# Sparse attention of a fp32 two-block network: scaled queries, fused add and minimum, row sums by a matmul column, head pairs as 64-row tiles

## The reference, cut to what matters

```python
q = rmsnorm(proj[..., :N_HEADS * dh].reshape(bsz, s, G, HG, dh), q_norm)
gates = jax.nn.sigmoid(proj[..., N_HEADS * dh:])
...
s_c = einsum('bghqd,bgnd->bghqn', qblk, k_c) * scale + head_bias(rel_c)   # 15 compressed keys
o_c = einsum(masked_softmax(s_c, rel_c >= 0), v_c)
...
s_s = einsum('bghqd,bgqkd->bghqk', qblk, k_sel) * scale + bias_s          # selected keys
p_s = masked_softmax(s_s, rel_s >= 0)
o_s = einsum('bghqk,bgqkd->bghqd', p_s, v_sel)
...                                                                       # window: the same with k_w, v_w
return gblk[..., 0:1] * o_c + gblk[..., 1:2] * o_s + gblk[..., 2:3] * o_w
```

## Time and profile before

| what | value |
|---|---|
| median of 3 runs | 1692.65 us |
| the profiled execution: its time, its span | 1695.91 us, 1694.1 us |
| PE busy over the span | 1623.7 us (96%) |
| attention stage from the first query chunk to the first wo_n matmul | 1360.3 to 1477.9 us |
| heads, from one pair to the next | 8.3 us |

### The profile page before, as it was taken

One profiled execution on the slowest core, in us unless ns is written; L12 is line 12 of the kernel. 1 busy time (PEld: TensorE's weight loads), 2 busy tenths in 40 slices (PEclk: granted clock), 3 DMA queues, 4 the chain that ended last, 5 costly groups with the idle time before them and its releaser, 6 DMA issues.

```text
span 1694.1 us, 33532 instructions
## 1 busy us (share of the span) xinstructions
PE 1623.7 (96%) x11620; PEld 1530.7 (90%) x11620; DVE 1096.8 (65%) x1762; ACT 885.5 (52%) x1468; POOL 182.8 (11%) x149
## 2 busy tenths in 40 slices
PE   5899999999999999999999999998999988799999
PEld 5689998977999889998999999888999867799997
DVE  5668666635776666666877666785566737676665
ACT  5476554444655445445446445554545547664443
POOL 5560000065100000000000000000000043300000
PEclk9899999989999999999999999998999989999999
DMA  5216556543465565556665555656455680055554
GB/s 199 87 51 185 184 178 195 166 155 129 160 196 182 186 196 178 184 185 192 195 189 183 187 181 184 203 183 196 150 185 185 202 173 26 1 171 182 181 190 145
DMA packets 81709, 282.80 MB, mean 167 GB/s; under 512 B 8800, under 2 KB 13408, under 8 KB 81632
## 3 DMA queue, kind: packets, MB, share of 16 engines
q1 hardware_dynamic: 77840, 276.88, 50.8%
q10 hardware_dynamic: 3792, 4.85, 1.6%
HBM read 280.12 MB, written 1.57 MB: 166 GB/s over the span
## 4 chain that ended last, share of the span: by engine, by line
PE 89%; DVE 4%; ACT 3%; issue 1%; DMA 1%; ACTq 1%; POOL 0%; SPq 0%; DVEq 0%; POOLq 0%
PE psum L1639 18%; PE psum L1641 18%; PE psum L1640 18%; PE psum L1631 16%; PE psum L1632 9%; PE psum L1767 2%; PE psum L1768 2%; PE psum L1769 2%; ACT arena L847 1%; DMA raw<-tiles 1%; PE psum L2022 1%; PE psum L1929 0%; DMA x<-x_in 0%; DVE arena L1510 0%; DVE xs L986 0%
## 5 line engine op out<-in xcount | busy, mean ns | idle before, releaser
L506 ACT ACTIVATE w_hi<-raw 128x1024 fp32r<-128x1024 f32 x522 | 549.8, 1055 | 479.8 <-PE psum L1641 298.4
L963 DVE TENSOR_TENSOR w_lo<-raw,w_hi 128x1024 fp32r<-128x1024 f32 x468 | 572.0, 1223 | 227.9 <-ACT w_hi L506 227.5
L1639 PE MATMUL psum<-xs,w_hi 128*128 128x256 f32 x1960 | 558.8, 285 | 16.2 <-DVE xs L986 16.2
L1640 PE MATMUL psum<-xs,w_hi 128*128 128x256 f32 x1960 | 556.8, 284 | 0.0
L1641 PE MATMUL psum<-xs,w_lo 128*128 128x256 f32 x1960 | 556.7, 284 | 0.0
L1631 PE MATMUL psum<-hs,w_hi 128*128 128x512 f32 x1216 | 421.8, 390 | 0.0
L1639 PEld LDWEIGHTS psum<-xs,w_hi 128*128 128x128 f32 x1960 | 378.3, 193 | 17.7 <-issue 11.2
L1640 PEld LDWEIGHTS psum<-xs,w_hi 128*128 128x128 f32 x1960 | 378.5, 193 | 0.2
L1641 PEld LDWEIGHTS psum<-xs,w_lo 128*128 128x128 f32 x1960 | 378.4, 193 | 0.0
L1632 PE MATMUL psum<-hs,w_lo 128*128 128x256 f32 x1216 | 342.9, 282 | 0.0
L1631 PEld LDWEIGHTS psum<-hs,w_hi 128*128 128x128 f32 x1216 | 228.3, 188 | 47.6
(11 more groups left out here) (280 smaller groups left out, 1636.6 us busy)
## 6 DMA issues: line engine op xcount, KB each, us to landing
raw<-tiles SPq DMA_DIRECT2D x522, 512.0 KB, 4.1
bias<-bias_dram ACTq DMA_DIRECT2D x8, 256.0 KB, 12.9
x<-x_in SPq DMA_DIRECT2D x1, 1024.0 KB, 8.2
y_out<-x SPq DMA_DIRECT2D x8, 128.0 KB, 3.4
con<-consts SPq DMA_DIRECT2D x1, 771.0 KB, 9.0
bias_dram<-bias_row ACTq DMA_DIRECT2D x1, 512.0 KB, 7.2
row<-rows SPq DMA_DIRECT2D x1, 192.0 KB, 9.2
vec<-vecs SPq DMA_DIRECT2D x1, 80.5 KB, 3.3
```

Source lines behind the costliest of these rows:

```text
L506: act.activation(w_hi[s][:, :], raw[s][:, :], ACT.Copy).then_inc(hi_ready, 1)
L963: dve.tensor_tensor(w_lo[s][:, :], raw[s][:, :], hi_of(w_hi[s][:, :]), ALU.subtract).then_inc(lo_ready, 1)
L1639: pe.matmul(out, w_hi[s][:, c:c + P], x_hi, start=first, stop=False)
L1640: pe.matmul(out, w_hi[s][:, c:c + P], x_lo, start=False, stop=False)
```

## The change

The loop is unrolled into 8 rounds k of two heads (e = 0, 1). Queries are scaled in place before they are turned, by minus the scale; the bias row is negated too, so logits come out negative: the maximum becomes a minimum and Exp takes scale -1. One `tensor_tensor_reduce` adds the bias and leaves the minimum, which is Exp's bias as it stands. `vtok` gets a 65th column of ones for each head and branch, so that the values matmul also gives the row sums; gate and row sum are applied to the output, not the probabilities. The zero-padded copies of the queries are gone: each head's scores use its own 64 rows of the array, e = 0 and e = 1 in turn, into different banks. The gates are Exp, add, reciprocal. POOL adds the branches' outputs. The compressed branch's turn and values, all of group 1's compressed branch and its `turn_queries` move into the rounds.

```diff
@@ gpsimd
-            with pool.Fori(0, HG) as i:
-                for w in range(4):
-                    pool.wait_ge(n_gs, i * 4 + (w + 1))
-                    ... pool.tensor_tensor(probs, probs, n_sc[w]..., ALU.mult) for 2 query blocks
+            for h in range(H):
+                pool.wait_ge(n_od, h + 1)
+                pool.tensor_tensor(both, br[:, :, 0, :], br[:, :, 1, :], ALU.add).then_inc(n_added, 1)
+                pool.wait_ge(n_co, 1 + h // 8)
+                pool.wait_ge(n_added, h + 1)
+                pool.tensor_tensor(no4[:, :, h, :], both, no4[:, :, h, :], ALU.add).then_inc(n_oo, 1)
@@ scalar: nsa
-                split(t0 + RING)
-                (gates: ACT.Sigmoid here)
-                for t in range(t0 + 1, t0 + 4):
+                for t in range(t0, t0 + 4):
                     split(t + RING)
+                def gates():
+                    act.wait_ge(n_gturn, 1)
+                    act.wait_ge(n_root, 1)
+                    (2 x ACT.Exp of 48 columns, scale=n_nr)
-                def queries(i, j):
-                    (4 copies of 64x256 for each two heads)
+                def exps(k, e):
+                    h = 2 * k + e
+                    act.wait_ge(n_log, h + 1)
+                    if k:
+                        act.wait_ge(n_pT, 2 * (h - 2) + 2)
+                    for tb, (a, z) in enumerate([(0, P), (P, 3 * P)]):
+                        for br in range(2):
+                            (ACT.Exp, scale=-1.0, bias=n_mn[h % 4][:, m:m + 1], no accum_out)
                 squares(0)
+                roots(0)
                 split(t0 + 4 + RING)
-                roots(0)
                 queries_turned(0)
+                for t in range(t0 + 5, t0 + 8):
+                    split(t + RING)
                 squares(1)
                 roots(1)
+                for k in range(H // 2):
+                    exps(k, 0)
+                    if k == 0:
+                        gates()
+                    exps(k, 1)
+                    if k in (0, 4):
+                        compressed_exps(k // 4)
+                    probs_turned(k, 0)
+                    probs_turned(k, 1)
+                    if k == 0:
+                        queries_turned(1)
+                    if k in (1, 4):
+                        compressed_turned(k // 4)
@@ vector: nsa
                 def query_scales(g):
+                    then(dve.reciprocal(n_r[...], std[...]))
+                    for tb in range(TB):
+                        dve.tensor_tensor(q, q, r.unsqueeze(2).to_broadcast([P, 8, DH]), ALU.mult).then_inc(n_scaled, 1)
+                def logits(k, e):
+                    h = 2 * k + e
+                    dve.wait_ge(n_s, k + 1)
+                    if k:
+                        dve.wait_ge(n_exp, h - 1)
+                    for tb, (a, z) in enumerate([(0, P), (P, 3 * P)]):
+                        for br in range(2):
+                            dve.tensor_tensor_reduce(out=n_l[e][...], in0=bank(2 * e + br, a, z), in1=table,
+                                                     scale=1.0, scalar=3.0e38, op0=ALU.add, op1=ALU.min,
+                                                     accum_out=n_mn[h % 4][:, m:m + 1])
-                (maxima: tensor_reduce x2, tensor_scalar; scales: reciprocal, tensor_tensor)
+                def outputs(k, e):
+                    dve.wait_ge(n_pv, h + 1)
+                    then(dve.reciprocal(ri.unsqueeze(2), pv[:, :, DH:]))
+                    then(dve.tensor_tensor(sc..., ri..., gate4[:, :, h, 1:3], ALU.mult))
+                    if h >= 4:
+                        dve.wait_ge(n_added, h - 3)
+                    dve.tensor_tensor(n_br[h % 4]..., pv[:, :, 0:DH], sc.unsqueeze(2)..., ALU.mult).then_inc(n_od, 1)
                 evacuate(1)
                 query_sums(1)
+                logits(0, 0)
+                logits(0, 1)
                 query_scales(1)
+                gates()
+                for k in range(H // 2):
+                    if k + 1 < H // 2:
+                        logits(k + 1, 0)
+                        logits(k + 1, 1)
+                    if k in (2, 5):
+                        compressed_outputs(k // 4)
+                    outputs(k, 0)
+                    outputs(k, 1)
+                    if k == 3:
+                        compressed_logits(1)
+                    if k in (1, 4):
+                        compressed_scales(k // 4)
@@ tensor: nsa
                 def turn_queries(g):
-                    pe.wait_ge(out_read, OUT0["nq"] + 2 * g + 2)
+                    pe.wait_ge(n_scaled, 2 * g + 2)
+                def scores(k):
+                    pe.wait_ge(n_qTd, 2 if k < 4 else 4)
+                    if k:
+                        pe.wait_ge(n_log, 2 * k)
+                    for br in range(2):
+                        for q0, q1, k1, at_ in ((0, P, P, 0), (P, S, S, P)):
+                            for e in range(2):
+                                rows = slice(e * DH, (e + 1) * DH)
+                                pe.matmul(bank(2 * e + br, at_, at_ + k1), n_qTa[rows, k * S + q0:k * S + q1],
+                                          kT[rows, key0:key0 + k1], start=True, stop=True)
+                def values(k, e):
+                    pe.wait_ge(n_pTd, 2 * h + 2)
+                    if k:
+                        pe.wait_ge(n_od, h - 1)
+                    if k in (2, 5):
+                        pe.wait_ge(n_co, 1 + k // 4)
+                    (6 matmuls of 65 columns: probabilities turned x vtok3[..., 64 values and a one])
-                between: 9 turn_queries(0), 11 compressed_scores(0), 13 compressed_turn(0), 15 compressed_values(0)
+                between: 12 turn_queries(0), 14 compressed_scores(0)
+                pe.wait_ge(out_read, OUT0["nq"] + 4)
+                scores(0)
+                for k in range(H // 2):
+                    turn_probs(k, 0)
+                    if k + 1 < H // 2:
+                        scores(k + 1)
+                    turn_probs(k, 1)
+                    if k in (2, 5):
+                        compressed_values(k // 4)
+                    values(k, 0)
+                    values(k, 1)
+                    if k == 0:
+                        turn_queries(1)
+                    if k in (1, 4):
+                        compressed_turn(k // 4)
+                    if k == 3:
+                        compressed_scores(1)
```

More of the change, by code:

```diff
@@ L364, in build @@
         n_qTa = part(6336, 2 * D)
-        n_qT = [[part(14720 + S * (2 * j + e), S) for e in range(2)] for j in range(2)]
+        n_br = [part(14720 + S * j, S) for j in range(4)]
+        n_sum2 = [part(15744 + P * j, P) for j in range(2)]
+        n_nr, n_nr8 = (part(16000 + 32 * j, TB) for j in range(2))
         n_l = [part(8896 + 768 * j, 768) for j in range(2)]
@@ L369, in build @@
         n_pTs = [part(11968 + 768 * j, 768) for j in range(2)]
-        n_mx, n_nmx, n_rs, n_sc = ([part(13504 + 16 * j + 4 * w, 4) for w in range(4)] for j in range(4))
+        n_mn, n_ri, n_sc = ([part(13504 + 16 * j + 4 * w, 4) for w in range(4)] for j in range(3))
         n_cl = [part(13568 + H * NC * tb, H * NC) for tb in range(TB)]
@@ L850, in probs_turned @@
[L850 to L855, removed]
+                def exps(k, e):
[5 more added lines that the diff above has]
+                        for br in range(2):
+                            m = 2 * tb + br
+                            ins = act.activation(n_p[e][:, br * 384 + a:br * 384 + z], n_l[e][:, br * 384 + a:br * 384 + z], ACT.Exp,
+                                                 scale=-1.0, bias=n_mn[h % 4][:, m:m + 1])
+                    ins.then_inc(n_exp, 1)
@@ L873, in nsa @@
[L873 to L888, removed]
@@ L1429, in nsa, with gates @@
                 no4 = no_tok.rearrange("p (t h d) -> p t h d", t=TB, h=H)
+                def gates():
+                    dve.wait_ge(n_gates, 1)
+                    then(dve.tensor_scalar(n_gate, n_gate, 1.0, None, ALU.add))
+                    then(dve.reciprocal(n_gate, n_gate))
                 def evacuate(g):
@@ L1530, in nsa @@
                 narrow("ngate", 3 * H)
-                for j in range(2):
-                    for e in range(2):
-                        ins = dve.memset(n_qT[j][e][DH - e * DH:P - e * DH, :], 0.0)
-                ins.then_inc(n_zero, 1)
+                dve.tensor_scalar(n_nr, rstd[:, 0:TB], -1.0, None, ALU.mult).then_inc(n_root, 1)
+                then(dve.tensor_scalar(n_nr8, rstd[:, 0:TB], -DH ** -0.5, None, ALU.mult))
                 dve.memset(n_cl[0], 0.0)
@@ L1959, in compressed_scores @@
                         pe.wait_ge(n_co, 1)
+                        pe.wait_ge(n_od, 7)
                     for j in range(4):
```

255 lines of the change are left out of this document (77 added, 178 removed).

## The result

The changed kernel took 1697.99 us (median of 15 runs, 1695.27 to 1702.81), the kernel before 1692.65 in runs of the same session (15 runs, 1691.05 to 1695.71). The ratio is 1.0028, with a 95% interval of 1.0020 to 1.0036: slower by about 5 us, where 1687.0 was forecast. The time lies above the range, which ended at 1696.

A forecast was written before the change was run, and what follows sets the result against it. PE was taken to bind, narrowly: start 1400.8 + rounds 44.2 + moved work 8.0 + waits 10.9 + clock 5.0 + end 3.2 = 1472.1 against 1477.93. The 5.8 us came off 1692.65: 1687, range 1677 to 1696.

The forecast's parts named there:

- Clock: 5.0 us: PE at half clock for 2.5 us behind four gaps (the start, rounds 0, 1, 4), 1.25 us each, 5.0 in all.
- Start: From projection to heads: PE idles 3.5 us, half clock until about 1391, first probabilities turned at 1400.8.
- Round: PE's round of two heads: turns, values without gain from 65 columns, scores 1.7; 5.7 us, eight rounds 44.2.
- The fused operation: DVE's add and minimum in one operation, taken at 1.3 us a head, between bounds of 1.13 and 2.9.
- New waits: PE waits for copies after rounds 0, 1, 4, for compressed outputs in 2, 5, and for gates: 10.9 us.
- one case for the clock, that it stays up: Rival: gaps don't lower the clock and loads of different row groups overlap; 1679, chance 0.16.
- The rival of tiles that don't overlap: Scores of a pair take 2.6 us, 6.3 more in all: 1693, with drains 1696; chance 0.17.
- The slow fused operation: Rival: add and minimum take 2.9 us a head, DVE's chain binds, 12 us more, 1699; chance 0.10.
- the cheap values: Rival: values of 65 columns take 0.7 us a head instead of 1.34; 3.5 us off, 1683; chance 0.07.
- The side "slower", 0.16: Chance that the whole kernel gets slower, made up of the slow fused operation and the tiles with drains.

The follow-up runs named there:

- The kernel with filled gaps: The changed kernel with all its waits, plus spare 128-column matmuls (result unused) in PE's gaps: 1684.99 us, ratio 0.9942 to the kernel before.
- wide values: The changed kernel with each values matmul moving 128 columns instead of 65: 1694.62 us, ratio 0.9999 to the kernel before.
- the order: The changed kernel with ACT making the next Exps before it copies turned queries or compressed probabilities: 1690.02 us, ratio 0.9979 to the kernel before.
- the kernel with the gaps closed by order: The changed kernel with Exps ahead of copies, compressed values ahead of the next scores, and first output chunks turned early: 1677.92 us, ratio 0.9898 to the kernel before.

## Why the prediction was wrong

The step that failed is **Clock: 5.0 us**. The other terms, one by one:

- *Start.* The first turn of probabilities was forecast for 1400.8 and came at 1398.83. PE ran out of work 2 us sooner (4.87 idle, not 3.5), and the half clock behind it ended at 1386.2 instead of 1391.
- *Round.* Values of 65 columns take 0.11 us an instruction, no gain, as forecast. Scores are 1.51 us from start to start at full clock (forecast 1.7), and the change into 64-row tiles costs 0.1 by the step from a turn to scores, 0.81, against 0.71 from a turn to values. An undisturbed round, the one from 1439.52, took 5.90 (5.7).
- *The fused operation.* 0.21 + 0.21 + 0.34 + 0.34 from start to start, 1.1 us a head; 1.3 was taken. The accumulator reads lie inside that.
- *New waits.* 2.54, 2.12 and 2.11 (2.8 and twice 2.3), 1.47 twice (1.5), nothing for the gates (0.5): 9.7 of 10.9.
- *Clock.* From the first turn of probabilities to wo_n the forecast had 1472.1 - 1400.8 = 71.3 us, or 66.3 without its 5.0 for the clock. The kernel with filled gaps, whose clock is 1.00, needs 1466.10 - 1399.51 = 66.6. The kernel after needs 1479.25 - 1398.83 = 80.4. All other terms together were thus right to 0.3 us, in part because small errors cancel (rounds a little longer, waits 1.2 shorter), and the clock cost 80.4 - 66.6 = 13.8.

The span came out at 1697.1 instead of 1688.3, 8.8 us longer: 9.1 between the first turn and wo_n (8.8 for the clock, 0.3 for the rest), 2.0 less by the sooner start, and 1.7 more behind the start of wo_n, which ran its first 2.4 us at half clock. The rest up to 11 us in the median is that the profiled execution before lay 3.3 above its median and the one after 0.9 above.

The mistake of reasoning: half clock was priced by one row, 2.5 us behind a gap, in which PE did mostly full-width work. The earlier trace rows also had 6.6 us at 0.50 behind the 5 us gap, and a good half of them were 30-column matmuls, as the kernel before shows:
```profile
1384.98 3.62 PE L1963 MATMUL psum<-kcT,arena 128*128 128x30 f32 x16 [5.01 <-ACT arena L816]
```
The prediction used that row for the projection and not for the rounds. The change put 64-row scores and 65-column values behind the gaps, and under these half clock lasted up to ten microseconds and began also after gaps of 1.47 us, where the 1.45 us gaps of the earlier trace rows had left the clock at 1.00. The rivals had one case for the clock, that it stays up, and none that it stays down. The rival of tiles that don't overlap was wrong: one head at a time takes 2.34 us against 1.58. The slow fused operation and the cheap values were wrong too. The side "slower", 0.16, came true by a mechanism that was not named.

Shown is: the gaps start most of the loss (shortening or closing them by order returns 8 and 22 us, filling them 14.6), the lightness prolongs it (wide values return 5 us, 6 on top of the order, and 37 where scores go one head at a time), and light matmuls put into the kernel before, with its own gaps, slow it. Not settled is what weight rows, columns and gaps have against each other. The 3.54 us gap ahead of round 0 left the scores behind it at 1.58 in the kernel with the Exps ahead and at 2.87 in the kernel after, so the same gap does not always have the same effect. Nor does the length of the half clock in one trace measure the work behind it: in the projection, where the same instructions follow, it lasted 3.0 us behind a gap of 4.87 in the kernel after, and 5.6 behind one of 5.61 in the kernel with the gaps closed by order. The medians of the runs carry the argument, and the traces say where the time went.

## What to carry to other kernels

When an edit narrows matmuls whose time hardly depends on their width (here 0.11 us an instruction at 65 columns and at 128), it saves next to nothing and may cost the clock: read the granted clock over the stretch, and price its fall with the matmuls that will stand there, not with those that do now. Before a wait is moved into a round, look at what is queued ahead of it; putting the next Exps ahead of the copies was worth 8 us, of which only 4 were the wait. A quick test for clock trouble is to fill PE's gaps with spare matmuls: if time falls, the clock was the loss, and closing the gaps by order can be worth more than the gaps are long, as it was here.

## What the runs showed of the hardware

- A granted clock of 0.53 over 130 us in which PE was busy 89%, with 64-row scores one head at a time and 65-column values; with 128-column values in as many instructions 0.88 (over the 85 us from the first scores to wo_n), and 1701 instead of 1738 us. The Trainium skill ("TensorE: Matmul & The Clock Gate", The HAM clock gate) says that the clock is set by how busy the array has been recently. The trace agrees for the idle gaps; here the kind of matmul counted as well as PE's busy time.
- Two 64-row fp32 tiles at work in turn: 16 score instructions in 1.58 us, against 2.34 when all of one tile come first. The Trainium skill ("TensorEngine Tiling (Array Packing)", Key Properties) has tiles run in parallel, and the times agree, but only when the instructions alternate.
- Add and minimum fused, with its accumulator: 287 ns for 128 columns and 420 for 256, at steps of 0.21 and 0.34 us, with 83 ns reads hidden under the next one.
